# Past keys loaded two rows to a partition, two pages to the halves of two places; values of a page on 64 partitions

## The chip, the cores and the metric

The kernel runs on one core of a Trainium2 chip. The core has a matrix engine (TensorE, PE), a vector engine (VectorE, DVE), a scalar engine (ScalarE, ACT), a general engine (GpSimd, POOL) and a queue engine (SyncE, SP) that here only issues DMA transfers. They share a working memory of 128 partitions; 16 DMA engines move data between it and the main memory. The metric is the device time of one execution in microseconds (us).

## What is computed

One layer of a decoder on 512 prompt tokens and 8 sequences of 8 new sample tokens. What matters here is the first of the two attentions of the samples, in which each sequence reads 4096 past keys and values through a page table:

```python
k_past = cache_k_diff[l][page_table].reshape(db, PAST_LEN, N_HEADS_DIFF, 2, HEAD_DIM)
v_past = cache_v_diff[l][page_table].reshape(db, PAST_LEN, N_HEADS_DIFF, DIFF_V_DIM)
s_past = jnp.einsum('bqhcd,bkhcd->bchqk', q, k_past) * SCALE
p = jax.nn.softmax(jnp.concatenate([s_past, s_new], axis=-1), axis=-1)
w = p[:, 0] - lam * p[:, 1]
o = einsum('bhqk,bkhe->bqhe', w[..., :p_len], v_past) + einsum('bhqk,bkhe->bqhe', w[..., p_len:], v_new)
```

A page is 128 tokens; the keys of a page are 128 rows of 512 floats (2 KB a row, 256 KB a page), and so are its values. 8 sequences of 32 pages make 256 key pages and 256 value pages. All rows of a page lie one behind the other in memory. The second attention of the samples reads a window of 2048 keys and values of 512 floats from a state, and the prompt has attentions of its own; these and the projections and the feed-forward part are as they were.

## The kernel before, in words

The attention of the samples is cut into 8 items (ITEMS). Items 0 to 3 are the paged attention, two sequences each; items 4 to 7 are the window attention. An item is a run of steps q: 8 steps for each of items 0 to 3 (steps 0 to 31), 3 for each of the others. A step of items 0 to 3 has 8 pages, i = 0 to 7: four of one sequence (half 0, i < 4) and four of the other (half 1). `FIRST[4]` is 32, the first step of the window attention. In the window attention, the third step of an item has only two pages to a half (`pages_of` is 2).

Keys come into `k_ring`, [128 partitions, 8 places, 512 floats], one place for each i. Before the change page i of a step is one DMA of 128 rows to 128 partitions of place i (line 768). DVE transposes each place by blocks of 32 x 32 into `kt_sb` (line 2153, `turn_page`), PE scores the queries against four pages at a time (line 1232, `score_keys`), and DVE copies the scores to `s_sb` (line 2190), which also puts the key columns into the order in which the values will lie. When an item's scores are complete, ACT takes the exponentials. The values follow LAG = 8 steps later: they come into `v_ring`, two halves of four pages (line 666, `place_values`); PE turns the probabilities (line 1245) and multiplies them with the values (line 1270, `weigh_values`). In the window attention `k_ring` and `kt_sb` (as `t_ring`) serve as further rings of values.

Before the change, value page k of a half goes to the 32 partitions k, k+4, k+8 and so on, four rows to each. In the window attention's short steps it goes to the 32 partitions k, k+2, ... below 64, four rows to each, which are there one run of 8 KB.

All these transfers stand on SP's one queue, in program order, with loads of weights and stores of results between them. In front of key page i of step t, SP waits until the transpose of page i of step t-1 has been done (`load_keys`, line 778); in front of four value pages of a half it waits until PE has weighed the four before them (`load_values`, line 792, `pv_half`). A key page so has one step of lead. The sequence on SP within a step is: key page 4 of the next step, four value pages of half 1, key pages 5, 6 and 7, key pages 0, 1 and 2 of the step after, four value pages of half 0, key page 3. Work of the prompt is strewn between the pages on every engine (`pieces`, `main`).

Where the diff says `key_load`, that is the page with whose transfer a page comes: itself in the paged attention, and the odd one of a pair in the full steps of the window attention, whose two key rows are adjacent and already come as one DMA of 4 KB rows.

## Time and profile before

| | |
|---|---|
| median of 3 runs | 1113.65 us (1112.84 to 1124.52) |
| the profiled execution | 1113.92 us, of which the span from first to last instruction is 1112.1 us |
| PE busy | 969.6 us, 87% of the span |
| DVE busy | 668.9 us, 60% |
| ACT busy | 505.7 us, 45% |
| POOL busy | 133.9 us, 12% |
| DMA moved | 310.98 MB, mean 280 GB/s |
| key pages of the cache | 256 transfers of 256 KB, 5.5 us from issue to landing |
| value pages of the cache | 256 transfers of 256 KB, 5.5 us |

A window row gives for a stretch of time the busy time of each engine, the TensorE clock that was granted (1 is full speed), the mean busy share of the 16 DMA engines and what they moved. A row of waits says which engine and line waited for which, the sum, the count and the longest. SPq is the issuing queue of SyncE: its time in a DMA instruction is the time to issue it, and longer where the DMA queues could take no more. A row of DMA issues ends with the median time from issue to landing. PE's busy time is no measure of work done, since matmuls are pipelined.

### The profile page before, as it was taken

Reading aid. Unit: us, or ns where it says so; the run is one execution under the profiler, and the core shown is the slowest. Engines: PE = TensorE matmul, PEld = TensorE weight load, DVE = VectorE, ACT = ScalarE, POOL = GpSimd, SP = SyncE. Lnnn points to the kernel's source line nnn. Section 1 sums busy time; section 2 is a strip of 40 time slices with the busy share of each in tenths; the row PEclk is TensorE's granted clock in tenths of the full one; section 3 lists DMA queues with packets and bytes.
Section 4 is the critical chain, followed back from the end, with each engine's and each line's share of the span. In section 5 each row is a group of like instructions: output and inputs, shape, how many; then the busy total and the mean of one; then the engine's idle time right before and its main releaser. Section 6 shows DMA issues by size and latency. Waiting matters only on the chain.

```text
span 1112.1 us, 29337 instructions
## 1 busy us (share of the span) xinstructions
PE 969.6 (87%) x11050; PEld 858.7 (77%) x11050; DVE 668.9 (60%) x1627; ACT 505.7 (45%) x1116; POOL 133.9 (12%) x69
## 2 busy tenths in 40 slices
PE   3989898998887779887889667899999999999995
PEld 3978787777764557676667554699999999999994
DVE  5389645675458887754346445788888888700003
ACT  5654543374125656645234262455555555611123
POOL 1322111111000010002111000000000000133330
PEclk8999999999988999888899787899999999999997
DMA  8699999999999999888979798386768686974632
GB/s 249 248 314 346 320 328 344 358 340 334 317 340 338 337 365 329 301 273 293 327 245 298 221 255 223 123 302 264 301 263 301 263 301 252 325 248 159 228 128 85
DMA packets 174933, 310.98 MB, mean 280 GB/s; under 512 B 13601, under 2 KB 87714, under 8 KB 173282
## 3 DMA queue, kind: packets, MB, share of 16 engines
q1 hardware_dynamic: 172898, 305.24, 80.3%
q10 hardware_dynamic: 1920, 4.20, 1.4%
q8 instruction: 74, 1.21, 0.4%
q14 instruction: 41, 0.34, 0.1%
HBM read 302.30 MB, written 73.92 MB: 338 GB/s over the span
## 4 chain that ended last, share of the span: by engine, by line
PE 32%; issue 30%; DMA 11%; SPq 11%; DVE 7%; ACT 7%; ACTq 0%; POOL 0%; DVEq 0%; POOLq 0%
PE ps L1383 11%; DMA v_ring<-in_cache_v_diff 6%; SPq L666 5%; PE ps L1038 5%; PE ps L1270 4%; PE ps L1232 4%; SPq L768 4%; DVE kt_sb L2153 2%; ACT q_st L1678 2%; PE ps L1189 2%; DMA k_ring<-in_state_v_win 2%; DMA k_ring<-in_cache_k_diff 2%; PE ps L1115 1%; DMA v_ring<-in_state_v_win 1%; ACT s_sb L1723 1%
## 5 line engine op out<-in xcount | busy, mean ns | idle before, releaser
L2153 DVE STREAM_TRANSPOSE kt_sb<-k_ring 128x512 f32<-128x512 f32 x336 | 220.5, 691 | 86.5 <-DMA k_ring<-in_cache_k_diff 37.4
L1270 PE MATMUL ps<-v_ring,pt_sb 128*32 128x128 f32 (+1 forms) x2496 | 98.8, 306 | 62.1 <-DMA v_ring<-in_cache_v_diff 49.3
L1270 PEld LDWEIGHTS ps<-v_ring,pt_sb 128*32 128x32 f32 (+1 forms) x2496 | 75.7, 121 | 78.1 <-issue 67.8
L1038 PE MATMUL ps<-h_hi,w_hi 128*128 128x288 f32 x384 | 124.4, 324 | 1.9 <-DVE h_lo L2006 1.9
L1038 PE MATMUL ps<-h_lo,w_hi 128*128 128x288 f32 x384 | 115.0, 299 | 0.0
L1038 PE MATMUL ps<-h_hi,w_lo 128*128 128x288 f32 x384 | 114.7, 299 | 0.0
L1232 PE MATMUL ps<-kt_sb,q_st 128*32 128x128 f32 (+1 forms) x2816 | 97.0, 281 | 10.2 <-DVE q_st L2163 4.6
L989 POOL TENSOR_TENSOR c_lo<-c_raw,c_hi 128x1408 fp32r<-128x1408 f32 x14 | 46.6, 3332 | 440.2 <-ACT c_hi L1781 440.2
L1232 PEld LDWEIGHTS ps<-kt_sb,q_st 128*32 128x32 f32 x2816 | 72.9, 114 | 28.2 <-issue 19.9
L1038 PEld LDWEIGHTS ps<-h_hi,w_hi 128*128 128x128 f32 x384 | 74.0, 193 | 16.1 <-issue 13.8
L949 POOL TENSOR_TENSOR w_lo<-w_raw,w_hi 128x1024 fp32r<-128x1024 f32 x24 | 57.3, 2390 | 229.5 <-ACT w_hi L1492 229.5
L1693 ACT ACTIVATE pt_sb<-ps 128x512 f32<-128x512 f32 (+1 forms) x44 | 26.2, 594 | 129.2 <-PE ps L1245 129.2
L1320 PE MATMUL ps<-t_h,s_h 128*128 128x288 f32 x264 | 77.9, 295 | 1.2 <-ACT u L1774 1.2
L1320 PE MATMUL ps<-t_l,s_h 128*128 128x288 f32 x264 | 77.9, 295 | 0.0
L1320 PE MATMUL ps<-t_h,s_l 128*128 128x288 f32 x264 | 77.7, 294 | 0.0
L2444 DVE TENSOR_TENSOR x<-x,ps 128x512 f32 (+1 forms) x8 | 5.5, 689 | 119.5 <-PE ps L1396 119.5
L2292 DVE TENSOR_TENSOR s_l<-s_t,s_h 128x512 fp32r<-128x512 f32 x88 | 58.8, 689 | 28.4 <-ACT s_h L1745 18.1
L1383 PE MATMUL ps<-a_hi,c_hi 128*128 128x288 f32 x352 | 75.4, 296 | 0.2 <-POOL c_lo L989 0.2
L1383 PE MATMUL ps<-a_lo,c_hi 128*128 128x288 f32 x352 | 75.3, 295 | 0.0
L1383 PE MATMUL ps<-a_hi,c_lo 128*128 128x288 f32 x352 | 74.9, 294 | 0.0
L1038 PEld LDWEIGHTS ps<-h_lo,w_hi 128*128 128x128 f32 x384 | 74.3, 194 | 0.0
L1038 PEld LDWEIGHTS ps<-h_hi,w_lo 128*128 128x128 f32 x384 | 73.9, 192 | 0.0
(236 smaller groups left out, 2289.4 us busy)
## 6 DMA issues: line engine op xcount, KB each, us to landing
k_ring<-in_cache_k_diff SPq DMA_DIRECT2D x256, 256.0 KB, 5.5
v_ring<-in_cache_v_diff SPq DMA_DIRECT2D x256, 256.0 KB, 5.5
out_k_win_sample<-in_state_k_win SPq DMA_DIRECT2D x32, 1020.0 KB, 8.3
out_v_win_sample<-in_state_v_win SPq DMA_DIRECT2D x32, 1020.0 KB, 8.5
k_ring<-in_state_k_win SPq DMA_DIRECT2D x32, 512.0 KB, 7.7
w_raw<-in_w_in SPq DMA_DIRECT2D x24, 512.0 KB, 6.3
g_raw<-in_w_gate SPq DMA_DIRECT2D x11, 1024.0 KB, 5.2
g_raw<-in_w_up SPq DMA_DIRECT2D x11, 1024.0 KB, 5.2
```

What stands on the lines that cost most here:

```text
L666: queue.dma_start(dst, src).then_inc((k_landed, v_landed, t_landed)[ring][i], 16)
L768: sp.dma_start(k_ring[:, at_first:i + 1, :].squeeze(1) if at_first == i else k_ring[:, at_first:i + 1, :], src)\
L949: nc.gpsimd.tensor_tensor(w_lo[:, n % 3, :], w_raw[:, n % 3, :], w_hi[:, n % 2, :].bitcast(F32), ALU.subtract).then_inc(w_lo_done, 1)
L989: nc.gpsimd.tensor_tensor(c_lo[j][:, 0:width], c_raw[:, j, 0:width], c_hi[j][:, 0:width].bitcast(F32), ALU.subtract).then_inc(w_lo_done, 1)
L1038: last = nc.tensor.matmul(M[c][:, 0:HALF], wt, act[:, k, c * HALF:(c + 1) * HALF], start=k == 0 and at_first, stop=k == KT - 1 and act is ...
L1232: last = nc.tensor.matmul(S[32 * f:32 * f + 32, c0:c0 + 32 * n], q_st[:, h, f, r, :], kt_sb[:, 4 * h:4 * h + n, c:c + 32], start=r % 2 == ...
L1270: last = nc.tensor.matmul(O[32 * f:32 * f + 32, P * h:P * h + P], pt_sb[0:rows, 4 * f + b, :], values[:, f * P:(f + 1) * P], start=g == 0 ...
L1320: last = nc.tensor.matmul(ps[:, bank, 0:HALF], wt[:, k, :], act[:, k, :], start=j in (0, 1, 3) and k == 0 and at_first, stop=k == 3 and wt ...
L1383: last = nc.tensor.matmul(main_ps[:, 2 * bank + c, 0:HALF], wt[j][:, w], a_lo[:, pair, block, :] if low else a_hi[pair][:, block, :], star ...
L1693: nc.scalar.activation(pt_sb[r].rearrange("p m (k t) -> p k m t", k=4), X[r].rearrange("p (k m t) -> p k m t", k=4, t=DT), ACT.Copy).then_ ...
L2153: V.transpose(kt_sb[:, i, :], k_ring[:, i, :]).then_inc(kt_done, 1)
L2292: V.tensor_tensor(dst[:, :, :], src, high[:, :, :].bitcast(F32), ALU.subtract).then_inc(form_low, 1)
```

## The change

Key pages of items 0 to 3: a page goes to 64 partitions, the lower ones for an even i and the upper ones for an odd i, with two adjacent rows (4 KB) to each partition, into the two places i and i+1 of a pair. A place of `k_ring` then holds every second row of two pages. DVE's transpose of either place so needs both pages of the pair; it writes the four places of a half in the order 0, 2, 1, 3, so that the score columns stand as before for all but the token order. SP may overwrite a pair only when both its transposes have been done.

Value pages of items 0 to 3: to keep the new token order, page k of a half goes to 64 partitions (every second one, from k // 2) and fills two of the four row slots there, with rows s and s + 64 of the page, where it went to 32 partitions and four slots. The window attention stays as it is.

```diff
         def place_values(queue, q, i, src):
             h, k = divmod(i, 4)
             n = pages_of(q)
-            if n == 4:
-                src = src.rearrange("(b j) c -> j b c", b=4)
-            rows, ring = slice(k, 32 * n, n), ring_of(q + LAG)
-            dst = (k_ring[rows, 4 * h:4 * h + 4, :], v_ring[rows, h, :, :], t_ring[rows, h, :, :])[ring]
+            ring = ring_of(q + LAG)
+            if q < FIRST[4]:
+                src = src.rearrange("(b s) c -> s b c", b=2)
+                rows, b = slice(k // 2, P, 2), slice(2 * (k % 2), 2 * (k % 2) + 2)
+            else:
+                if n == 4:
+                    src = src.rearrange("(b j) c -> j b c", b=4)
+                rows, b = slice(k, 32 * n, n), slice(0, 4)
+            dst = (k_ring[rows, 4 * h + b.start:4 * h + b.stop, :], v_ring[rows, h, b, :], t_ring[rows, h, b, :])[ring]
             queue.dma_start(dst, src).then_inc((k_landed, v_landed, t_landed)[ring][i], 16)
...
-                    at_first = i - (it >= 4 and n == 4)
-                    sp.dma_start(k_ring[:, at_first:i + 1, :].squeeze(1) if at_first == i else k_ring[:, at_first:i + 1, :], src)\
-                        .then_inc(k_landed[i], 16)
+                    if it < 4:
+                        rows = slice(64 * (i % 2), 64 * (i % 2) + 64)
+                        dst, src = k_ring[rows, i - i % 2:i - i % 2 + 2, :], src.rearrange("(p r) c -> p r c", r=2)
+                    else:
+                        dst = k_ring[:, i - 1:i + 1, :] if n == 4 else k_ring[:, i, :]
+                    sp.dma_start(dst, src).then_inc(k_landed[i], 16)
...
-                        sp.wait_ge(kt_done, PAGE_NO[last, i] + 1 if i % 4 < pages_of(last) else half_end(last, h))
+                        sp.wait_ge(kt_done, PAGE_NO[last, i | 1] + 1 if i % 4 < pages_of(last) else half_end(last, h))
...
-                at_load = key_load(t, i)
-                dve.wait_ge(k_landed[at_load], K_LANDS[t, at_load])
+                for page in (i - i % 2, i | 1) if t < FIRST[4] else (key_load(t, i),):
+                    dve.wait_ge(k_landed[page], K_LANDS[t, page])
                 if t:
                     dve.wait_ge(scored if i >= 4 else half_scored, t)
-                V.transpose(kt_sb[:, i, :], k_ring[:, i, :]).then_inc(kt_done, 1)
+                to = i - i % 4 + (0, 2, 1, 3)[i % 4] if t < FIRST[4] else i
+                V.transpose(kt_sb[:, to, :], k_ring[:, i, :]).then_inc(kt_done, 1)
```

On SP's queue, in the middle of the paged attention (two key pages and the first value pages of a half, after a load of `w_raw`), before:

```order
L768 ISA [waits kt_done]
L768 DMA k_ring<-in_cache_k_diff 128x512
L756 TENSOR_LOAD page_ids [waits pv_half0]
L666 ISA
L666 DMA v_ring<-in_cache_v_diff 32x4x512
L666 ISA
L666 DMA v_ring<-in_cache_v_diff 32x4x512
```

and in the changed kernel at the same place:

```order
L778 ISA [waits kt_done]
L778 DMA k_ring<-in_cache_k_diff 64x1024
L762 TENSOR_LOAD page_ids [waits pv_half0]
L672 ISA
L672 DMA v_ring<-in_cache_v_diff 64x2x512
L672 ISA
L672 DMA v_ring<-in_cache_v_diff 64x2x512
```

No transfer is added, taken away or moved; the shapes differ, 64 partitions of 4 KB for keys and 64 of 2 x 2 KB for values.

On DVE, the transposes of one step (second half of a step, then first half of the next), before:

```order
L2153 STREAM_TRANSPOSE kt_sb<-k_ring 128x512 [waits scored,k_landed5]
L2153 STREAM_TRANSPOSE kt_sb<-k_ring 128x512 [waits scored,k_landed6]
L2153 STREAM_TRANSPOSE kt_sb<-k_ring 128x512 [waits scored,k_landed7]
L2153 STREAM_TRANSPOSE kt_sb<-k_ring 128x512 [waits half_scored,k_landed0]
L2153 STREAM_TRANSPOSE kt_sb<-k_ring 128x512 [waits half_scored,k_landed1]
```

and in the changed kernel:

```order
L2164 STREAM_TRANSPOSE kt_sb<-k_ring 128x512 [waits scored,k_landed5,k_landed4]
L2164 STREAM_TRANSPOSE kt_sb<-k_ring 128x512 [waits scored,k_landed7,k_landed6] x2
L2164 STREAM_TRANSPOSE kt_sb<-k_ring 128x512 [waits half_scored,k_landed1,k_landed0] x2
L2164 STREAM_TRANSPOSE kt_sb<-k_ring 128x512 [waits half_scored,k_landed3,k_landed2] x2
```

The transposes stand where they stood; each of the first of a pair now also waits for the second page.

## Rows read from the trace of the kernel before

**Rows 1.** Windows, whole core; columns are named in the first row.
```profile
core 0: us, PE busy (x) PEld busy (x) DVE busy (x) ACT busy (x) POOL busy (x), PEclk, DMA share, GB/s
60.00:130.00 70.00, 63.98 (x870) 57.42 (x871) 60.82 (x166) 33.21 (x71) 14.36 (x6) 0.98 1.01 336
130.00:200.00 70.00, 64.12 (x934) 56.07 (x933) 37.63 (x95) 28.76 (x57) 11.91 (x5) 0.98 0.99 331
200.00:300.00 100.00, 86.61 (x1294) 74.74 (x1293) 56.63 (x151) 43.71 (x92) 16.53 (x7) 0.97 1.00 337
...
345.00:440.00 95.00, 77.48 (x1241) 56.67 (x1241) 79.66 (x278) 60.31 (x189) 7.01 (x12) 0.96 0.98 345
```

**Rows 2.** Waits of all engines from 60 to 440 us, longest in total first.
```profile
DVE s_sb L2190 <- PE ps L1232: 42.9, 24, 5.0
...
DVE kt_sb L2153 <- DMA k_ring<-in_cache_k_diff: 37.4, 28, 2.7
PE ps L1270 <- DMA v_ring<-in_cache_v_diff: 37.1, 24, 4.1
```

**Rows 3.** Waits of the DMA-issuing queue SPq from 60 to 440 us.
```profile
SPq L768 <- DVE kt_sb L2153: 10.4, 14, 3.0
...
SPq L666 <- PE ps L1270: 2.1, 1, 2.1
```

**Rows 4.** Chain that ended last from 60 to 440 us, its shares by line.
```profile
by line: SPq L666 14.3%; PE ps L1038 13.0%; SPq L768 10.2%; DMA v_ring<-in_cache_v_diff 10.2%; issue 8.9%; PE ps L1232 7.8%; DMA k_ring<-in_cache_k_diff 4.7%; PE ps L1270 4.7%; DVE kt_sb L2153 4.1%; SPq L756 2.6%; ACT q_st L1678 2.1%; PE ps
```

**Rows 5.** DMA transfers at 447 to 449.5 us (four-kilobyte rows among them).
```profile
DMA packets 412, 1.00 MB, mean 400 GB/s; under 512 B 46, under 2 KB 46, under 8 KB 412
...
k_ring<-in_state_k_win SPq DMA_DIRECT2D x3, 512.0 KB, 7.3
```

**Rows 6.** DMA transfers at 117 to 122 us (key pages of two-kilobyte rows).
```profile
DMA packets 1098, 1.99 MB, mean 398 GB/s; under 512 B 128, under 2 KB 136, under 8 KB 1097
...
k_ring<-in_cache_k_diff SPq DMA_DIRECT2D x7, 256.0 KB, 5.6
```

**Rows 7.** DMA transfers at 2.7 to 4.2 us (mostly four-kilobyte rows).
```profile
DMA packets 168, 0.62 MB, mean 415 GB/s; under 512 B 16, under 2 KB 16, under 8 KB 168
```

**Rows 8.** Windows late in the window attention, columns as in group 1.
```profile
641.00:647.00 6.00, 2.20 (x44) 2.05 (x48) 1.60 (x3) 5.94 (x17) 0.00 (x0) 0.50 1.03 196
648.00:654.00 6.00, 5.29 (x66) 4.08 (x55) 2.01 (x7) 2.38 (x5) 0.00 (x0) 0.83 1.03 192
655.00:660.00 5.00, 4.12 (x94) 3.29 (x89) 4.82 (x9) 2.76 (x7) 0.00 (x0) 1.00 1.07 373
662.00:669.00 7.00, 3.23 (x73) 2.29 (x71) 2.57 (x3) 5.22 (x7) 0.00 (x0) 1.00 1.01 191
670.00:676.00 6.00, 5.86 (x87) 4.37 (x89) 4.90 (x14) 0.96 (x3) 0.00 (x0) 0.54 1.06 387
```

**Rows 9.** DMA transfers at 648 to 654 us.
```profile
DMA packets 473, 1.15 MB, mean 192 GB/s; under 512 B 73, under 2 KB 73, under 8 KB 419
...
v_ring<-in_state_v_win SPq DMA_DIRECT2D x2, 256.0 KB, 15.2
```

**Rows 10.** DMA instructions on SPq by line: duration ns min/median/max.
```profile
L768 SPq DMA_DIRECT2D k_ring<-in_cache_k_diff x256: 332/333/2361, 21.5 to 439.7; - x128
L666 SPq DMA_DIRECT2D v_ring<-in_cache_v_diff x256: 602/602/2186, 53.8 to 572.1; - x128
L666 SPq DMA_DIRECT2D v_ring<-in_state_v_win x36: 482/603/1672, 579.2 to 672.4; - x36
L714 SPq DMA_DIRECT2D x<-in_x_sample x2: 471/523/575, 3.5 to 696.0; - x2
L814 SPq DMA_DIRECT2D out_k_diff_sample<-ks x1: 549/549/549, 115.9 to 115.9; - x1
```

**Rows 11.** Page part 6: issues, KB each, median us to landing.
```profile
k_ring<-in_cache_k_diff SPq DMA_DIRECT2D x256, 256.0 KB, 5.5
```

**Rows 12.** Transposes at line 2153 from 60 to 440 us.
```profile
L2153 DVE STREAM_TRANSPOSE kt_sb<-k_ring x247: 667/702/715, 59.6 to 438.5; 128x512 f32<-128x512 f32 x124
```

## Prediction, made before the changed kernel ran

> **What bounds the kernel now.** I read the windows by stage first. From 60 to 440 us, where the 256 key pages and most value pages of the cache are read, the DMA engines are busy 98 to 101% of the time and move 331 to 345 GB/s, while PE is busy 82 to 92% of each stretch [rows 1]. So two things are nearly full at once, and a stage like that has no slack for slower transfers. The waits agree: the transposes wait 37.4 us for key pages and the value product 37.1 us for value pages [rows 2]; SP itself waits little for the buffers, 10.4 us for transposes in front of key pages and 2.1 us for PE in front of value pages [rows 3]. The chain of that stretch says what the latency is made of: SP issuing value pages 14.3%, SP issuing key pages 10.2%, value pages on their way 10.2%, key pages on their way 4.7%, against 13.0% for the projection and 12.5% for PE's scores and value products [rows 4]. The reader is to see that the transfers and their issue hold some 40% of that chain, and that the DMA engines have no idle time from which a slower page could be paid.
>
> The sum is made against the profiled execution: 1113.9 us with a span of 1112.1 us. The median of the runs, 1113.65 us, is the same within 0.3 us, so what is added to one is added to the other.
>
> **The change, part by part.**
>
> *Longer rows for keys.* A key page becomes 64 rows of 4 KB instead of 128 of 2 KB. Where full queues carry 2 KB key rows, they move 398 GB/s [rows 6]; where nearly all rows are of 4 KB, 415 GB/s [rows 7]; with both kinds mixed, 400 GB/s [rows 5]. 262,144 bytes take 0.659 us at 398 and 0.632 us at 415 GB/s: 0.027 us a page, 7 us for 256 pages, if every page lies on the path. Bounds: 0 and -7 us. I take -5.
>
> *Fewer partitions for each key page.* This is the part that decides. A page now goes to the lower or the upper 64 partitions only. The trace has transfers that do so in a full queue: the short steps of the window attention load value pages to 32 partitions, all below 64, in runs of 8 KB. At 641 to 647, 648 to 654 and 662 to 669 us, with such pages in the queue, the DMA engines are just as busy (1.01 to 1.03) but move 196, 192 and 191 GB/s; between them, at 655 to 660 and 670 to 676 us, when pages go to all partitions, 373 and 387 GB/s [rows 8]. In the second of these stretches only 54 of 473 packets are of 8 KB or more, and the smaller ones are slowed along with them, since 192 GB/s is the rate of all; such a page took 15.2 us to land [rows 9]. Engines that are busy all the time at half the rate wait inside their transfers, and what these stretches have beyond the others is transfers to one half of the partitions. They have another thing, runs of 8 KB, which the change does not bring; rows of 4 KB are not slow [rows 7], so I hold the half responsible. The new key pages go to one half each.
>
> The price: a page at the mean of the three slow rows (193 GB/s) takes 1.36 us, at the 338 GB/s of the stretch [rows 1] 0.78 us. That is 0.58 us more; 247 transposes, and so as many pages, fall between 60 and 440 us [rows 12]: 143 us. What speaks for less: consecutive key pages alternate between the halves, so that an engine that has run ahead by one page writes to the other half than its partner, and the two do not collide. The slow rows had no such alternation. If leads are random, half of the loss is avoided, 72 us; if they arrange themselves, all of it. A store from 64 partitions, at 115.9 us [rows 10], shows no dent at 117 to 122 us [rows 6], but that is one transfer of half the size. What speaks for more: in the slow rows pages that go to all partitions were slowed too; if the value pages between the key pages were, the loss would be about twice 143 us. Bounds: 0 and +286 us. Nothing in a common queue that all engines empty in order makes them take turns, and a full queue that is limited by its writes gives them little to drift apart by, so I take three quarters of the full price, +107 us.
>
> The Trainium skill speaks against this change on this point ("SBUF — State Buffer", Door 1: The DMA port swizzle): partitions 0 to 63 reach only 8 of the 16 ports, the same as 0 to 31, and two concurrent transfers to partition 0 and partition 64 came out only 6% faster than one. It gives 196 GB/s for 0 to 63 at 1 MiB, beside the 191 to 196 GB/s of this trace; an estimate from its figure for every key page would be +139 us, and its 6% leaves hardly anything to the alternation. By that page the sum would be some 32 us higher than mine.
>
> *SP's issue.* SP needs 0.333 us for a key page to 128 partitions. For 64 partitions of 4 KB it took 0.471 and 0.575 us, and for a store from 64 partitions 0.549 us [rows 10]. So a key page costs SP 0.14 us more (bounds 0 and 0.24), 1.1 us for a step's eight. A value page to 32 partitions takes 0.602 us with four pieces, 0.482 us at least with one; 64 partitions with two pieces lie between, so 0 to -0.12 us, and I take -0.03. The chain holds 10.2% of 380 us = 39 us of key issue [rows 4]; times 0.14/0.333 that is +16 us, less 54 us x 0.03/0.602 = 3 us: +13 us if the queues stay as they are. If pages move at half rate the DMA queues stay full and SP has time, so beside the +107 us I count 0 to 13 and take +4.
>
> *The pair wait.* A transpose waits for both pages of its pair, and SP overwrites an even place one transpose later. The second page was issued right behind the first, 0.5 us later, and a transpose takes 0.70 us [rows 12]. Hidden by a lead of one step (380 us / 31 steps = 12 us) against 5.5 us to landing [rows 11]. Were this cover gone, the first transpose of each of four pairs would start up to 0.7 us late in each of 31 steps, at most +87 us, with the value pages queued behind SP's wait and PE's scores behind DVE. SP's 10.4 us of such waits in 380 us [rows 3] say that it is near 0; with slow pages it hides nothing more than what is already counted. I take 0, bound +10.
>
> *Work elsewhere.* The transposes, scores, copies and value products are as many and as large as before: 0.
>
> Sum: -5 + 107 + 4 + 0 = +106 us, 1113.9 + 106 = 1220 us.
>
> **The rivals.**
>
> *Slower, by half-rate key pages:* the forecast, 70%. Its own range goes from half the price less the gain for longer rows (+36 to +72, so 1150) to the full price with issue and some of the value pages slowed (1295).
>
> *Faster:* engines drift apart by a page, each half of the partitions is then written by half of the engines, and only the longer rows count, -7 us in rate and perhaps as much again from key and value pages that land sooner. Issue must then not be on the path. This gives 1100 to 1107 us. For it speaks the store that left no dent [rows 6, 10]; against it, the slow rows and 13 us of issue. It decides for faster if a key page costs no more than 0.33 us on SP and the stretch stays over 345 GB/s. 12%.
>
> *Slower by SP alone:* no collision, but +13 us for issue and up to +10 for the pair wait, less 5: 1120 to 1132 us. The point from which it decides is an issue time above 0.45 us. 9%.
>
> *No difference:* the gain of the rows and the cost of the issue cancel, or PE at 82 to 92% busy is the true limit: 1106 to 1120 us. 9%.
>
> **How the numbers follow.** The predicted time is 1220 us. The range reaches from 1110 to 1290: it leaves out the faster case (12%), a small part of no difference, and about 5% above. The likeliest case's own range is 1150 to 1295. About 1% is what a measurement of this kernel can tell from no change. Slower by over 1% is the forecast and most of SP alone, 0.78; within 1%, 0.10; faster by over 1%, 0.12.
>
> **What would show it.** Right: windows from 60 to 440 us (then longer) with the DMA share near 1 and 200 to 280 GB/s; key pages landing in 8 us or more instead of 5.5; waits of line 1270 for value pages and of the transposes for key pages well above 37 us each; PE's share of that stretch below 80%, perhaps with a granted clock lower than 0.98; no change after the stretch. Issue: 0.47 us for a key page on SP. Wrong: 340 GB/s or more with key pages on 64 partitions would mean that the engines do take turns, and the time would then be near or below 1113 us. If the rate holds and SP fills the chain, it was the issue. If the rate is below 200 GB/s throughout, value pages were slowed too and the time goes beyond the range.

## The result: 13 to 14% slower, nearly all of it while the key pages are loaded

| | us |
|---|---|
| before, median of 7 runs | 1113.74 |
| changed kernel, median of 7 runs | 1279.76 (1253.25 to 1288.32) |
| ratio to before | 1.128, 95% interval [1.122, 1.133] |
| the same kernel again, beside the experiments | 1266.02 (1246.50 to 1269.01); ratio 1.139 [1.134, 1.143] |
| predicted | 1220, range 1110 to 1290 |

Some executions of the changed kernel are 1 to 2% longer than the others; the ratios are meant to leave them out, but the second one is not what its two short executions give (1246.50 and 1264.96 us, 1.127 of the mean before). I compare by ratios; 1% of the kernel before is 11.1 us. The change costs +142 us by the first ratio and +154 us by the second; the truth may lie anywhere between, and the second is the less certain of the two. The profile shown is of an execution of 1246.50 us, the shortest of the second comparison. In the changed kernel line 778 loads keys (768 before), 672 values (666), 2164 transposes (2153), 1279 is the value product (1270), 1241 the scores (1232), 762 a read of page ids on SP (756).

The same stretches as in [rows 1], in the changed kernel:

```profile
core 0: us, PE busy (x) PEld busy (x) DVE busy (x) ACT busy (x) POOL busy (x), PEclk, DMA share, GB/s
60.00:130.00 70.00, 55.05 (x658) 48.26 (x659) 47.16 (x123) 24.74 (x43) 11.94 (x5) 0.88 1.05 249
130.00:200.00 70.00, 53.70 (x714) 47.06 (x712) 30.10 (x88) 25.67 (x64) 9.44 (x4) 0.85 1.06 243
200.00:300.00 100.00, 74.91 (x954) 63.97 (x944) 46.26 (x118) 30.23 (x58) 11.71 (x5) 0.83 1.07 259
345.00:440.00 95.00, 63.94 (x841) 51.44 (x842) 37.37 (x114) 15.23 (x39) 2.34 (x1) 0.80 0.99 248
```

The DMA engines are as busy as before, 0.99 to 1.07, but move 243 to 259 GB/s where they moved 331 to 345. PE falls from 82 to 92% of a stretch to 67 to 79% (63.94 of 95, 55.05 of 70 us), and beside its idle time the granted clock falls from between 0.96 and 0.98 to between 0.80 and 0.88.

The waits from 60 to 440 us, all engines (what was waited for, sum, count, longest); they answer to [rows 2]; those of ACT and POOL are left out:

```profile
DVE kt_sb L2164 <- issue: 126.3, 60, 7.0
...
PE ps L1279 <- DMA v_ring<-in_cache_v_diff: 76.8, 23, 5.6
...
DVE kt_sb L2164 <- DMA k_ring<-in_cache_k_diff: 23.2, 9, 4.0
...
PEld ps L1241 <- DVE kt_sb L2164: 6.7, 11, 3.5
...
DVE kt_sb L2164 <- PE ps L1241: 4.7, 2, 3.5
PE ps L1241 <- DVE kt_sb L2164: 4.3, 2, 3.3
```

The value product waits 76.8 us for value pages, where it waited 37.1 us. The transposes have 126.3 us of idle time, which this view puts down to no releaser ("issue"), and 23.2 us for key pages; before it was 37.4 us for key pages. That the 126.3 us are key pages too is an inference, from the chain of the stretch, [rows 4] then and this line now:

```profile
by line: DMA k_ring<-in_cache_k_diff 26.2%; SPq L778 15.6%; SPq L672 14.2%; issue 13.1%; DMA v_ring<-in_cache_v_diff 7.1%; PE ps L1047 3.8%; SPq L762 2.7%; DVE kt_sb L2164 2.7%; PE ps L1241 1.8%; SPq L827 1.4%; DVE feat L2035 1.3%; PE ps L1
```

Key pages on their way hold 26.2% of the chain (4.7% before), their issue 15.6%, the issue of values 14.2%. The projection, 13.0% before, holds 3.8%: in that stretch PE is no longer what the end waits for.

The DMA instructions of line 778 and 672 on SP (shortest, median, longest in ns; then the start of the first and of the last, us), which answer to [rows 10], and the landing times of the page's part 6, which answer to [rows 11]:

```profile
L778 SPq DMA_DIRECT2D k_ring<-in_cache_k_diff x256: 468/475/5792, 21.8 to 565.0; - x128
```

```profile
L672 SPq DMA_DIRECT2D v_ring<-in_cache_v_diff x256: 604/615/2547, 54.2 to 711.7; - x128
```

```profile
k_ring<-in_cache_k_diff SPq DMA_DIRECT2D x256, 256.0 KB, 9.8
v_ring<-in_cache_v_diff SPq DMA_DIRECT2D x256, 256.0 KB, 9.6
```

The last key page is issued at 565.0 us instead of 439.7 [rows 10]: 125.3 us of the 132.6 us between the two spans (1244.7 and 1112.1) are lost by then. From there to the end it takes 679.7 us, 672.4 before. A page lands in 9.8 us instead of 5.5, and value pages, which go to every second partition of all 128, in 9.6 us: they suffer with the keys. SP waits longer for the transposes, which are late themselves (10.4 us in [rows 3]):

```profile
SPq L778 <- DVE kt_sb L2164: 36.9, 24, 3.4
SPq L762 <- DVE kt_sb L2164: 27.9, 15, 6.1
```

### The profile page after: what moved, and what is told of

It reads as the page before. It is cut to its first block, busy times and chain, and to the rows that moved or that the text cites. A ratio compares the mean times of both kernels' runs of the same rounds, so it can differ in the third digit from the quotient of the medians.

```text
span 1280.1 us, 29345 instructions
## 1 busy us (share of the span) xinstructions
PE 1023.2 (80%) x11050; PEld 899.0 (70%) x11050; DVE 671.6 (52%) x1627; ACT 506.5 (40%) x1116; POOL 133.4 (10%) x69
## 4 chain that ended last, share of the span: by engine, by line
issue 29%; DMA 26%; PE 19%; SPq 17%; DVE 6%; ACT 2%; POOL 0%; ACTq 0%; DVEq 0%; POOLq 0%
DMA k_ring<-in_cache_k_diff 17%; PE ps L1392 10%; SPq L672 8%; SPq L778 5%; DMA v_ring<-in_cache_v_diff 4%; PE ps L1047 2%; DVE kt_sb L2164 2%; PE ps L1279 2%; DMA v_ring<-in_state_v_win 2%; DMA k_ring<-in_state_v_win 2%; DMA k_ring<-in_state_k_win 2%; SPq L762 1%; PE ps L1198 1%; ACT q_st L1687 1%; PE ps L1241 1%
## 5 line engine op out<-in xcount | busy, mean ns | idle before, releaser
L1279 PE MATMUL ps<-v_ring,pt_sb 128*32 128x128 f32 (+1 forms) x2496 | 110.9, 332 | 164.2 <-DMA v_ring<-in_cache_v_diff 150.5
L1279 PEld LDWEIGHTS ps<-v_ring,pt_sb 128*32 128x32 f32 (+1 forms) x2496 | 85.5, 132 | 181.0 <-issue 175.4
L1047 PE MATMUL ps<-h_hi,w_hi 128*128 128x288 f32 x384 | 129.8, 338 | 1.9 <-DVE h_lo L2015 1.9
L1241 PE MATMUL ps<-kt_sb,q_st 128*32 128x128 f32 (+1 forms) x2816 | 108.0, 303 | 15.6 <-DVE kt_sb L2164 5.1
L1047 PE MATMUL ps<-h_lo,w_hi 128*128 128x288 f32 x384 | 119.5, 311 | 0.0
L1047 PE MATMUL ps<-h_hi,w_lo 128*128 128x288 f32 x384 | 118.6, 309 | 0.0
L1241 PEld LDWEIGHTS ps<-kt_sb,q_st 128*32 128x32 f32 x2816 | 81.2, 124 | 37.4 <-issue 21.1
L1047 PEld LDWEIGHTS ps<-h_hi,w_hi 128*128 128x128 f32 x384 | 78.3, 204 | 18.4 <-issue 16.1
L1702 ACT ACTIVATE pt_sb<-ps 128x512 f32<-128x512 f32 (+1 forms) x44 | 26.2, 595 | 137.3 <-PE ps L1254 137.3
L1047 PEld LDWEIGHTS ps<-h_lo,w_hi 128*128 128x128 f32 x384 | 78.8, 205 | 0.0
L1047 PEld LDWEIGHTS ps<-h_hi,w_lo 128*128 128x128 f32 x384 | 78.2, 204 | 0.0
```

Of the source, the lines that this page charges most:

```text
L1047: last = nc.tensor.matmul(M[c][:, 0:HALF], wt, act[:, k, c * HALF:(c + 1) * HALF], start=k == 0 and at_first, stop=k == KT - 1 and act is ...
L1241: last = nc.tensor.matmul(S[32 * f:32 * f + 32, c0:c0 + 32 * n], q_st[:, h, f, r, :], kt_sb[:, 4 * h:4 * h + n, c:c + 32], start=r % 2 == ...
L1279: last = nc.tensor.matmul(O[32 * f:32 * f + 32, P * h:P * h + P], pt_sb[0:rows, 4 * f + b, :], values[:, f * P:(f + 1) * P], start=g == 0 ...
L1702: nc.scalar.activation(pt_sb[r].rearrange("p m (k t) -> p k m t", k=4), X[r].rearrange("p (k m t) -> p k m t", k=4, t=DT), ACT.Copy).then_ ...
```

## The experiments

One number holds much of what follows: what the DMA engines move from 60 to 440 us. This is the line of the kernel before and that of the changed one:

```profile
DMA packets 85838, 128.36 MB, mean 338 GB/s; under 512 B 7466, under 2 KB 29098, under 8 KB 85777
```

```profile
DMA packets 55993, 95.62 MB, mean 252 GB/s; under 512 B 5551, under 2 KB 27183, under 8 KB 55950
```

The same 128.36 MB at 252 GB/s take 510 us instead of 380, +130 us; the spans differ by 132.6 us. For each experiment the same two numbers, from its own profiled execution (that of keys two and two took 1289.67 us):

| kernel | MB in these 380 us | time for 128.36 MB, less 380 us | its span less 1112.1 us | ratio of the runs |
|---|---|---|---|---|
| changed | 95.62 | +130 | +132.6 | 1.139 |
| keys on every second partition | 118.71 | +31 | +37.4 | 1.030 |
| keys in halves, old values | 92.41 | +148 | +163.1 | 1.142 |
| only the pair waits | 124.00 | +13 | +14.6 | 1.012 |
| only the new value shape | 128.79 | -1 | -1.2 | 1.001 |
| a tiny transfer for every second key page | 117.86 | +34 | +31.7 | 1.031 |
| stores issued by ACT | 130.53 | -6 | -13.6 | 0.992 |
| keys in halves, two and two | 89.37 | +166 | +175.8 | 1.146 |
| keys in halves, pieces of 2 KB | 95.34 | +132 | +146.5 | 1.143 |
| values in halves, in turn | 105.40 | +83 | +154.2 | 1.139 |
| values in halves, two and two | 100.28 | +106 | +189.7 | 1.171 |

Where the keys, the waits or the issue were changed, most of the time is lost as the rate of this one stretch. Where the values go in halves, little more than half of it is: their pages are loaded until 720 us and later, far behind 440. Of the 13.6 us that the stores on ACT win in their profiled execution, 6 are won here. Where keys or values lie at other tokens than in the reference, the text on record says so; the sizes and counts are the same.

**Which partitions.** One line of the changed kernel differs: a key page goes to 64 partitions still, in rows of 4 KB still, but to every second partition instead of one half.

```diff
-                        rows = slice(64 * (i % 2), 64 * (i % 2) + 64)
+                        rows = slice(i % 2, P, 2)
```

> The changed kernel, but key page i goes to every second partition (0, 2, 4, ... or 1, 3, 5, ...) instead of to the lower or upper 64. Still 64 partitions of 4 KB, two places a pair, the same waits, the same value layout. (The keys of a page so lie at other tokens than its values; every transfer and operation is as in the changed kernel.) Theory (pages to one half of the partitions collide): the DMA engines go back to over 330 GB/s at 60 to 440 us, the time comes to 1105 to 1135 us. Rival (64 partitions, 4 KB rows, SP's longer issue or the pair wait cost the time): stays within 2% of the changed kernel's 1257 us.

1150.30 us (1147.29 to 1151.25), ratio 1.030 [1.025, 1.035]. Its windows (columns as above, in all that follow), and its key issues on SP:

```profile
60.00:130.00 70.00, 62.96 (x817) 56.10 (x818) 53.77 (x142) 27.03 (x48) 14.34 (x6) 0.93 0.92 302
130.00:200.00 70.00, 61.14 (x865) 53.77 (x867) 37.03 (x98) 31.89 (x73) 11.43 (x5) 0.93 0.96 326
200.00:300.00 100.00, 84.20 (x1256) 72.60 (x1245) 56.52 (x153) 43.83 (x92) 14.60 (x7) 0.98 0.95 315
345.00:440.00 95.00, 68.49 (x1028) 49.17 (x1028) 74.53 (x254) 47.26 (x155) 5.38 (x8) 0.86 0.93 312
```

```profile
L778 SPq DMA_DIRECT2D k_ring<-in_cache_k_diff x256: 474/489/1387, 22.2 to 471.1; - x128
```

The rate is 302 to 326 GB/s instead of 243 to 259, and the issue time is nearly that of the changed kernel (489 and 475 ns). Number of partitions, row length, waits and the order of the transfers are all the same. Which 64 partitions a page is written to makes 0.098 to 0.109 of the kernel before, 109 to 121 us. That is shown, not argued. The rate and the time did not come as far back as I had expected (over 330 GB/s, 1105 to 1135 us): 33 us are left against the kernel before. The chain from 60 to 440 us:

```profile
by line: SPq L672 24.6%; SPq L778 22.8%; issue 17.4%; DMA k_ring<-in_cache_k_diff 15.6%; SPq L762 5.4%; DVE kt_sb L2164 2.5%; SPq L701 2.1%; PE ps L1047 1.8%; SPq L827 1.4%; SPq L815 1.2%; DVE prob L2054 1.1%; PE ps L1241 1.1%; SPq L835 0.6
```

SP's two issue lines hold 47.4% of it (24.5% before), and the DMA share in the windows is 0.92 to 0.96. By this chain the kernel is held up more by SP's queue than by the DMA engines.

**The keys alone, the values alone.** First the changed kernel with the old value loads, then the kernel before with the new ones.

```diff
-            if q < FIRST[4]:
-                src = src.rearrange("(b s) c -> s b c", b=2)
-                rows, b = slice(k // 2, P, 2), slice(2 * (k % 2), 2 * (k % 2) + 2)
...
+            if n == 4:
+                src = src.rearrange("(b j) c -> j b c", b=4)
+            rows, ring = slice(k, 32 * n, n), ring_of(q + LAG)
...
```

> Keys as in the changed kernel, on halves; values as before, 32 partitions of four rows. (Values lie at other tokens than the probabilities.) Theory: the keys alone make the loss, 1240 to 1280 us. Rival (the new value layout takes a good part of it): under 1220 us.

1274.35 us (1271.66 to 1277.04, 2 runs), ratio 1.142 [1.134, 1.150]: as much as the whole change.

```diff
-            if n == 4:
-                src = src.rearrange("(b j) c -> j b c", b=4)
-            rows, ring = slice(k, 32 * n, n), ring_of(q + LAG)
...
+            if q < FIRST[4]:
+                src = src.rearrange("(b s) c -> s b c", b=2)
+                rows, b = slice(k // 2, P, 2), slice(2 * (k % 2), 2 * (k % 2) + 2)
...
```

> Keys as before, 128 partitions of one row; values as in the changed kernel, 64 partitions of two rows. (Values lie at other tokens than the probabilities.) Theory: 1110 to 1120 us, SP's issue of a value page 0.60 to 0.62 us. Rival (the value layout is part of the loss): over 1140 us.

1116.18 us (1112.41 to 1126.89), ratio 1.001 [0.997, 1.005]. The value edit changes the time by less than 0.5% either way; its issue time, in the line that follows, is the old 0.60 us.

```profile
L671 SPq DMA_DIRECT2D v_ring<-in_cache_v_diff x256: 604/605/1984, 55.1 to 573.4; - x128
```

**The pair waits alone.** The kernel before, whose transfers stay, with the two waits of the change: a transpose waits for both pages of its pair, SP for both transposes.

```diff
-                        sp.wait_ge(kt_done, PAGE_NO[last, i] + 1 if ...)
+                        sp.wait_ge(kt_done, PAGE_NO[last, i | 1 if t < FIRST[4] else i] + 1 if ...)
...
-                dve.wait_ge(k_landed[at_load], K_LANDS[t, at_load])
+                for page in (i - i % 2, i | 1) if t < FIRST[4] else (key_load(t, i),):
+                    dve.wait_ge(k_landed[page], K_LANDS[t, page])
```

> The kernel before with the pair waits alone: a transpose waits for both pages of its pair, SP overwrites an even place only after the odd one has been transposed. Theory: hidden, 1113 to 1118 us. Rival (the pair wait costs): 1125 us or more, with waits of the transposes for key pages well over 37 us from 60 to 440 us.

1128.47 us (1126.51 to 1133.81), ratio 1.012 [1.007, 1.018], so +14 us (7 to 20). I had expected the waits to be hidden; the rival's time, 1125 us or more, came instead. SP's waits for the transposes (sum, count, longest), the idle time of the transposes, and two windows:

```profile
SPq L768 <- DVE kt_sb L2153: 17.5, 16, 3.1
SPq L756 <- DVE kt_sb L2153: 13.0, 20, 2.4
```

```profile
DVE kt_sb L2153 <- issue: 70.5, 42, 3.9
...
DVE kt_sb L2153 <- DMA k_ring<-in_cache_k_diff: 11.7, 8, 3.7
```

```profile
60.00:130.00 70.00, 64.37 (x830) 57.76 (x831) 56.57 (x149) 29.70 (x58) 14.33 (x6) 0.93 0.94 310
...
200.00:300.00 100.00, 84.96 (x1250) 72.71 (x1252) 56.92 (x147) 44.23 (x92) 16.50 (x7) 0.97 0.97 327
```

SP waits 17.5 + 13.0 us for transposes, where it was 10.4 + 7.7 us before ([rows 3] show the first), and the DMA share falls from 1.01 to 0.94 and from 1.00 to 0.97 in these two. So the pair waits open gaps in the queue: 12 us more of waits on SP are not made up afterwards. With two pages to wait for, this view puts most of the transposes' idle time down to "issue" here too (70.5 us, and 11.7 us to key pages, where 37.4 us stood to key pages before). Which of the two waits costs the time, SP's or the transposes', was not taken apart.

**SP's issue time by itself.** The kernel before, and in front of every second key page a transfer of 4 bytes to a buffer of its own that nothing reads.

```diff
+                    if it < 4 and i % 2:
+                        n_extra[0] += 1
+                        c = n_extra[0] - 1
+                        sp.dma_start(extra[64:65, c:c + 1], consts[0:1, C_ID + c:C_ID + c + 1]).then_inc(extra_in, 16)
```

> The kernel before with one more tiny transfer (4 bytes to one partition) ahead of every second key page of the cache: about 0.33 us of SP's issue for two pages, 0.16 us a page, which is what a key page on 64 partitions costs more; it moves next to nothing. Theory (SP's issue is next to full): 15 to 40 us slower than before, SP lines taking over the chain from 60 to 440 us. Rival (the DMA queues are full, issue is hidden): under 8 us slower.

1147.53 us (1142.80 to 1149.76), ratio 1.031 [1.026, 1.036], +35 us (29 to 40). SP's time for them (ns, shortest, median, longest), and two windows:

```profile
L775 SPq DMA_DIRECT2D extra<-in_consts x128: 258/322/534, 22.9 to 475.6; - x128
```

```profile
130.00:200.00 70.00, 58.72 (x894) 51.11 (x894) 34.88 (x90) 29.24 (x60) 11.86 (x5) 0.98 0.95 311
...
345.00:440.00 95.00, 70.65 (x1004) 50.04 (x996) 72.58 (x248) 46.20 (x153) 4.66 (x8) 0.82 0.92 310
```

128 issues of 0.322 us are 41 us. The DMA share falls to 0.95 and 0.92 in these two, so the DMA engines now have gaps. Of the 41 us added on SP, 35 (29 to 40) came out as time of the kernel. SP's lines did not take the chain over, as I had written; they hold 31.9% of it (27.1% before), and key pages on their way 12.9% (4.7%). Whether a transfer of 4 bytes costs anything but its issue this run can't say; the next one takes the issue away instead.

**Less issue on SP.** The kernel before, in which ACT issues the stores of the new keys and values. The functions `store_k` and `store_group` and their calls go from SP's program to ACT's, behind the evacuations that write what is stored.

```diff
...
-                sp.dma_start(dst[:, :, (T % 4) * P:(T % 4 + 1) * P], k_stage[:, n % 2, :, :]).then_inc(k_stored[n % 2], 16)
...
+                act.dma_start(dst[:, :, (T % 4) * P:(T % 4 + 1) * P], k_stage[:, n % 2, :, :]).then_inc(k_stored[n % 2], 16)
...
```

> The kernel before with one change: the stores of the prompt's and the samples' new keys and values (28 transfers between 60 and 440 us) are issued by ACT, directly behind the evacuation that they wait for anyway, and no longer by SP between the pages. Nothing that is loaded, and no bytes, change. Theory that SP's issue time is exposed (the run with one tiny transfer per two key pages lost 34 us for about 41 us of added issue time): the 28 issues took SP roughly 0.5 us each, 14 us together, so 8 to 12 us come back, 1102 to 1106 us. Rival, that the added transfers of that run cost by their landing and completion, and not by the time on SP's queue: no difference beyond 3 us, 1110 to 1117 us. A third: ACT, now holding the issues, delays the prompt's evacuations on which PE waits: slower, 1118 us or more.

1106.28 us (1099.85 to 1110.59, 12 runs, against 1115.23 of the kernel before, 17 runs), ratio 0.992 [0.989, 0.995]: 6 to 12 us faster, and so the fastest of all the kernels here. The transfers from 60 to 440 us and two windows:

```profile
DMA packets 86880, 130.53 MB, mean 343 GB/s; under 512 B 7582, under 2 KB 29214, under 8 KB 86818
```

```profile
130.00:200.00 70.00, 64.28 (x934) 56.03 (x934) 38.02 (x95) 28.95 (x58) 11.86 (x5) 0.98 0.99 336
200.00:300.00 100.00, 89.17 (x1365) 77.22 (x1368) 59.07 (x154) 44.70 (x95) 16.57 (x7) 1.00 1.03 355
```

343 GB/s instead of 338 (the first of the two windows 336 instead of 331, the second 355 instead of 337). Together the two runs show that what stands on SP's queue costs time in the old arrangement although the DMA share is near 1, and that the share alone does not say so. SP was not full by its own records: from 60 to 440 us its instructions in the trace of the kernel before add up to 306 us, 249 of them in 477 DMA instructions, and its waits to 21 us. The stores also left SP's queue for another one here, and what that is worth by itself was not tested.

**Halves two and two.** The changed kernel, but pages 0 and 1 of four go to the lower half and 2 and 3 to the upper one, so that keys don't alternate page by page. The waits and the value pages follow and are not shown.

```diff
...
-                        rows = slice(64 * (i % 2), 64 * (i % 2) + 64)
-                        dst, src = k_ring[rows, i - i % 2:i - i % 2 + 2, :], src.rearrange("(p r) c -> p r c", r=2)
+                        rows, place = slice(64 * (k // 2), 64 * (k // 2) + 64), 4 * h + 2 * (k % 2)
+                        dst, src = k_ring[rows, place:place + 2, :], src.rearrange("(p r) c -> p r c", r=2)
...
```

> As the changed kernel, but pages 0 and 1 of a half step go to the lower 64 partitions and 2 and 3 to the upper, so that two pages in a row go to one half of the partitions instead of one; the value pages follow, so that the result is the same. Theory (pages to one half collide, and the alternation saves a part of it because engines drift apart by a page): slower than the changed kernel by 15 us or more, its rate below 235 GB/s from 60 to 440 us. Rival (the alternation saves nothing, or it is the drift between any two transfers): within 10 us of the changed kernel.

1286.19 us (1267.18 to 1290.52), ratio 1.146 [1.136, 1.156], beside 1.139 [1.134, 1.143] and 1.128 [1.122, 1.133] of the changed kernel: 8 to 20 us more, where one expectation had 15 us or more and the other 10 or less. The intervals of 1.146 and 1.139 overlap, and a transpose here waits for pages that are issued further apart as well. What the alternation is worth was not settled by it. In this and the next run the profile from 60 to 440 us has 235 and 251 GB/s, 252 in the changed kernel; the 235 are from an execution of 1289.67 us.

**Halves with short rows.** The changed kernel, with rows s and s + 64 on a partition, two pieces of 2 KB instead of one of 4 KB.

```diff
-... src.rearrange("(p r) c -> p r c", r=2)
+... src.rearrange("(r p) c -> p r c", r=2)
```

> As the changed kernel, with each partition getting rows p and p + 64 of the key page (two pieces of 2 KB) instead of two adjacent rows (one of 4 KB). (The keys of a page so lie at other tokens than its values.) Theory (the half of the partitions makes the loss, whatever the rows): within 25 us of the changed kernel, 1250 to 1285 us. Rival (rows of 4 KB are what collides): under 1200 us.

1269.21 us (1260.38 to 1276.32), ratio 1.143 [1.137, 1.148].

The issue of its key pages on SP:

```profile
L778 SPq DMA_DIRECT2D k_ring<-in_cache_k_diff x256: 598/604/6082, 21.7 to 579.6; - x128
```

SP needs 0.13 us more for each of 256 key pages, 33 us in all, and the time grows by 4 us over 1.139, by 17 over the first measurement of the changed kernel, 1.128; the intervals of 1.143 and 1.139 overlap. Where the pages are slow, about half or less of SP's added issue comes out as time (4 to 17 of 33 us); where they are fast, most of it does (35 of 41 us).

**The half of the partitions by itself.** What was missing was a price of the halves with no pair wait and no change in the issue time. The values can give it: keys as before, and the two-piece value pages of the run with ratio 1.001, sent to one half of the partitions each; once in turn, once two and two. The two diffs that follow are against that run, the first of them in turn:

```diff
-                rows, b = slice(k // 2, P, 2), slice(2 * (k % 2), 2 * (k % 2) + 2)
+                rows, b = slice(64 * (k % 2), 64 * (k % 2) + 64), slice(2 * (k // 2), 2 * (k // 2) + 2)
```

> Keys as in the kernel before, with its single-page waits. The value pages of the cache go to 64 partitions with two pieces each as in the run with old keys and new values (1116 us), but to the lower half for an even page and the upper half for an odd one, in place of every second partition. The values so lie at other tokens than the probabilities; sizes and counts are the same. This prices the half of the partitions with no pair wait and no change of SP's issue time beside it. Theory that the alternation buys nothing, so that a page costs the full 0.58 us more: 178 value pages in the stretch of full DMA engines make 103 us, the 78 after it 45 us less some 13 us of idle DMA time there, together +135 us on 1116: 1251 us, and the DMA rate from 60 to 440 us near 250 GB/s. Rival, that the alternation saves a third (0.39 us a page, from the two profiles of the changed kernel and of the one with keys on every second partition, 1244.7 and 1149.5 us): 69 + 30 - 13 = +86, 1202 us, and near 270 GB/s.

1273.38 us (1262.66 to 1284.00), ratio 1.139 [1.127, 1.151]. Against 1.001 that is +154 us (about 13 either way), 0.60 us for each of 256 value pages, 22 us more than the time I had expected. Windows:

```profile
60.00:130.00 70.00, 63.23 (x836) 56.80 (x836) 59.99 (x164) 32.10 (x68) 14.35 (x6) 0.95 1.02 331
130.00:200.00 70.00, 57.38 (x784) 49.75 (x785) 32.31 (x78) 25.09 (x54) 9.44 (x4) 0.90 1.04 276
200.00:300.00 100.00, 72.07 (x976) 61.17 (x975) 46.37 (x122) 40.26 (x81) 14.05 (x6) 0.88 1.06 256
345.00:440.00 95.00, 63.77 (x885) 47.09 (x873) 56.27 (x188) 32.62 (x107) 0.00 (x0) 0.84 1.06 260
440.00:560.00 120.00, 81.14 (x1112) 60.78 (x1112) 65.08 (x227) 46.82 (x136) 9.34 (x16) 0.82 1.02 244
```

The waits for key and value pages, 60 to 440 us:

```profile
PE ps L1275 <- DMA v_ring<-in_cache_v_diff: 74.8, 27, 6.4
DVE kt_sb L2158 <- DMA k_ring<-in_cache_k_diff: 74.5, 37, 5.1
...
DVE kt_sb L2158 <- PE ps L1237: 27.3, 12, 5.0
```

The landing times there (last column, us), and the issues of the value pages on SP:

```profile
k_ring<-in_cache_k_diff SPq DMA_DIRECT2D x209, 256.0 KB, 8.5
v_ring<-in_cache_v_diff SPq DMA_DIRECT2D x138, 256.0 KB, 10.2
```

```profile
L671 SPq DMA_DIRECT2D v_ring<-in_cache_v_diff x256: 598/599/3347, 54.6 to 719.5; - x128
```

This profile has its own control. From 60 to 130 us 69 key pages are issued, to all partitions, and only 2 value pages, and the rate is 331 GB/s (336 before). When the value pages with their halves come in, it is 276, 256 and 260 GB/s at a DMA share of 1.04 to 1.06. Key pages, untouched, land in 8.5 us instead of 5.5, and the transposes wait 74.5 us for them instead of 37.4. The issue takes the old 0.60 us, and the last value page is issued at 719.5 us instead of 572.1: 147 us later. Over the whole of 60 to 440 us the rate is 277 GB/s; my theory had said near 250 and the rival near 270, so in rate the rival was nearer, and in time (1251 and 1202 us) the theory. The first 70 us, nearly without value pages, are part of that: they lift the mean of the rate.

The same with two and two, against the same run:

```diff
-                rows, b = slice(k // 2, P, 2), slice(2 * (k % 2), 2 * (k % 2) + 2)
+                rows, b = slice(64 * (k // 2), 64 * (k // 2) + 64), slice(2 * (k % 2), 2 * (k % 2) + 2)
```

> As the run with value halves in turn, but pages 0 and 1 of four go to the lower half and pages 2 and 3 to the upper one, so that two transfers to the same half follow each other. The values again lie at other tokens. If the alternation buys nothing, the same time as with halves in turn within 5 us. If it saves a third of the price, this run loses some of that: 15 to 45 us above the other.

1303.58 us (1303.53 to 1312.29), ratio 1.171 [1.163, 1.179]. Windows, from 130 us on:

```profile
130.00:200.00 70.00, 49.96 (x695) 43.13 (x699) 29.05 (x74) 24.22 (x52) 9.46 (x4) 0.89 1.04 246
200.00:300.00 100.00, 69.70 (x958) 60.48 (x950) 45.56 (x122) 35.33 (x73) 11.71 (x5) 0.87 1.04 241
345.00:440.00 95.00, 63.19 (x799) 48.05 (x799) 42.24 (x140) 19.51 (x61) 2.34 (x1) 0.77 1.06 248
440.00:560.00 120.00, 72.16 (x986) 52.30 (x984) 65.84 (x218) 47.34 (x149) 6.99 (x12) 0.81 1.05 225
```

Two and two is 2.8% = 36 us slower than in turn (20 to 52 us by the two intervals), and the intervals do not touch. Against 1.001 it is +190 us, 0.74 us a value page. Alternation is worth something: 256 against 241 GB/s from 200 to 300 us, 6%. The Trainium skill ("SBUF — State Buffer", the question whether one can issue two DMAs to hit both halves) has +6% for two concurrent transfers to partition 0 and partition 64 over one. It is not quite the same comparison, but the gain here is of that size. My expectation had tied two things together that are not: that the alternation helps, and that the page then costs less than the full price. It does help, by some 0.14 us a page (0.08 to 0.20), and the page in turn still costs 0.60 us, which I had taken for the full price of a page without alternation. That full price was too low: two and two, which still changes halves every second page, already costs 0.74 us. That is for values; for keys the run above gives 8 to 20 us, 0.03 to 0.08 us a page.

## Why the prediction was right in sign and within its range, and where it was off

*What bounds the kernel: half right.* I read DMA engines without idle time and a chain with some 40% of transfers and issue [rows 1, 4], and concluded that slower pages must show in full. They did: the rate of that stretch fell to 252 GB/s, and that gives +130 of the +132.6 us between the two profiled executions. What I did not see is that SP's issue cost time beside them. The rows had it (24.5% of the chain in the two issue lines, 14.9% in pages on their way), but I let the DMA share near 1 overrule it.

*Fewer partitions, +107 us: mechanism right, size too small.* The price was 0.58 us a page from late stretches at 193 GB/s [rows 8], 143 us in full, and I took a quarter off for the alternation, 0.145 us a page. Measured by itself on the values, the page in turn costs 0.60 us, 154 us in all, and two and two 0.74 us. So with values the alternation saves 0.14 us a page, about what I took off; I had no row for it, so that it fits is luck. With keys the same two kernels are 142 to 154 us and 162 us (1.146) above the one before, 0.55 to 0.60 us and 0.63 us a page: the saving is smaller there, though other waits differ too. In both the full price of a page was set too low: 0.58 us from [rows 8], where two and two measured 0.63 and 0.74 us. That is the mis-sized term; for keys the quarter taken off was too much besides. The 247 pages instead of 256 are only 4 us of the miss. Why [rows 8] gave too little stays open. They show 192 GB/s as the rate of a mix, with only 54 of 473 packets of 8 KB or more [rows 9], and I used it as the rate of the half pages alone. With keys, against every second partition, the halves cost 109 to 121 us; that is perhaps less than 154 because the kernel it is taken from loses 33 us to issue and pair waits, which slow pages may hide. The Trainium skill ("SBUF — State Buffer", Door 1) stood in the prediction with an estimate of +139 us; it was nearer than mine to the measured +142 and +154.

*Runs of 8 KB are not needed for the loss: right.* Rows of 4 KB and pieces of 2 KB to one half lose about the same (1.128 to 1.139, and 1.143), and rows of 4 KB to every second partition do not. What the 8 KB runs did in [rows 8] itself was not tested.

*Longer rows, -5 us: not seen.* Halves with rows of 4 KB and with pieces of 2 KB differ by 4 to 17 us, all of which may be issue. With keys on every second partition the rows are long too and the kernel is at 1.030. That run has the pair waits (+14 by themselves) and 0.15 us more issue a key page, which at the rate of the tiny transfers (35 us for 41) would be some 33 us; 14 + 33 is more than its 33, so up to 14 us might be a gain from longer rows, or the two costs may hide each other. That was not taken apart.

*SP's issue: duration right, its value not.* 0.475 us for a key page, as I had from 0.471 [rows 10]. For the case of unchanged queues I had +13 us from the share of the chain; tiny transfers of about the same time cost 35 us, so the share of the chain was too low here: it counts what stands on the path now, not what comes onto it when it grows. Beside slow pages I had +4, and there 33 us more issue cost 4 us (17 against the first measurement), so 36 us more would be 4 to 18: at the low end. The value page was 0.604 us, so the -0.03 was 0.

*The pair wait, 0, bound +10: alone it is +14 (7 to 20).* I had set a lead of one step against the landing time. But SP's queue is behind the wait, and what SP lost there was not made up (12 us more of its waits, 14 us of time); the 10.4 us of waits in [rows 3], which I read as a sign of nearly nothing, were no small thing. In the changed kernel this cost seems to be hidden and not added: halves of values without it cost as much as the whole change (1.139). So the 0 of my sum stood, but by the slow pages and not by the lead that I gave as the reason; that is luck.

*The sum.* Predicted -5 + 107 + 4 + 0 = +106; measured +142 and +154. By the runs the halves alone make +154, taken on the values; that the same holds for the keys, and that the other edits so add nothing beside them, is an inference from equal page sizes and equal totals, since keys in halves without pair waits were not run. On it the miss of 36 to 48 us is all in the price of a page, 0.435 us after the quarter, where 0.55 to 0.60 us was measured. The range up to 1290 held it, since the likeliest case's own range went beyond that full price, to 1295.

*The rivals.* Drift, faster: excluded by the rate. SP alone, 1120 to 1132: it is what happens when the halves are taken away, 1150, and was underpriced by 18 to 30 us. No difference, through PE as the limit: excluded, PE's share fell. Of what was to show it, the DMA share near 1 with 200 to 280 GB/s, landing above 8 us, PE below 80% and a lower clock came as written; the idle time of the transposes was there, but the view of waits named the key pages for only 23.2 of its 149.5 us. No change after the stretch: 7 us, 679.7 against 672.4 us from the last key page to the end.

## What to carry to other kernels

Before a load is reshaped, one should ask which partitions each transfer writes: pages that went to only the lower or the upper 64 held the whole queue here to 243 to 259 GB/s instead of 331 to 345, with rows of 4 KB and with pieces of 2 KB, and although the halves alternated; pages on every second partition left it at 302 to 326, with SP's queue as the next limit. A DMA share near 1 does not clear the queue that issues: here 24.5% of the stretch's chain in its two issue lines was enough for moving 28 stores to ACT to gain 9 us, and for a wait or an issue added in front of the loads to cost nearly its full length. Where an earlier stretch of the same trace is to price a pattern, ask what else was in its queue: a rate of a mix is not the price of the one pattern in it.

## What the hardware showed that I had not expected

- The issue time on SP goes by shape and not by bytes: for 256 KB, 128 partitions of one row 0.333 us [rows 10], 64 partitions of 4 KB 0.475 and 0.489 us, 64 partitions of two pieces 0.599 to 0.615 us, 32 partitions of four pieces 0.602 us [rows 10]. A transfer of 4 bytes took 0.322 us, hardly less than a page.
- One half of the partitions slows the whole queue: in the run with value halves, key pages to all partitions went from 5.5 to 8.5 us to landing (60 to 440 us).
- In turn against two and two is worth about 6% of the rate (256 and 241 GB/s from 200 to 300 us), while the same pages spread over all partitions have 338 GB/s there (the run with only the new value shape).
